# Attention scores whose second pass is made of 64-row products on alternating halves of the rows

## The chip, the cores and the metric

The kernel runs on one core of a Trainium2 chip. Its engines run side by side and wait for each other through semaphores: TensorE multiplies matrices (a weight load, then a product that streams the other operand through it), VectorE and ScalarE work on elements, GpSimd works on elements and starts some transfers, SyncE starts most transfers. The metric is device microseconds from start to end, the median of three runs.

## The reference

Three transformer layers on 512 tokens of width 1024: a retention layer, a layer of chunk attention and a hybrid layer, with squared-ReLU and gated MLPs between them. The change touches the attention of the second and third layer, in which each head's query and key have 64 features:

```python
# layer 2, 16 heads: own chunk of 64 tokens and the 8 before
s = jnp.einsum('bqhd,bkhd->bhqk', qb, kb).astype(jnp.float32) * scale + bias[None]
p = jax.nn.softmax(s, axis=-1).astype(vb.dtype)
return jnp.einsum('bhqk,bkhd->bqhd', p, vb)
# layer 3, 4 heads with relative bias, 4 with a forget gate, 8 with a window of 128
lg = jnp.einsum('bhqd,bhqkd->bhqk', qb, kg).astype(jnp.float32) * SCALE
```

All of it is in float32. The last line stands for the three branches of the hybrid layer, which differ in mask and bias.

## The kernel before

**Number format.** A float32 value is split into a high part that TensorE takes in its f32r type and a low part, the rest. A product is made of three: high by high, high by low, low by high. ScalarE makes the high part (a copy into an f32r tile), VectorE the low part (the value less its high part).

**The work.** Units of 128x1024 weights stream in through a ring of four buffers; `split` makes their high and low parts (ScalarE L1278, VectorE L1919) and `proj` multiplies them (24 products of 128x512, L617 to L619). In the attention stage (the trace shows it from 805 to 965 us) one step of a loop handles several heads at different places of the pipeline. The second block (1372 to 1520 us) has the 16 heads of the hybrid layer in the same manner.

**One head.** `proj` gives a tile of q or k for a pair of heads, 64 rows each; `qk_tile` (VectorE L2473) brings it to `af`. For half 0 or 1 of the pair `q_hi` (ScalarE L1596) writes q's high part to the half's own 64 rows of `q_st`, and `q_lo` (VectorE L2480) its low part to the other 64. `k_hi` (L1602) writes k's high part to both halves of `kh_st`, and `k_lo` (L2487) its low part to the own half of `kl_st`, whose other half `zero_rows` has set to zero once. So in `scores` one product of 128 rows against `kh_st` (L956) is high by high plus low by high, and a second against `kl_st` (L957) adds high by low, with zeros for 64 of its rows. This is done for four query tiles of 128 tokens, each with the keys it can see: 128, 256, 384 and 512 wide in full heads, 128, 256, 256 and 256 in the window heads, two products a tile, one after the other. Heads 4 to 7 of the second block add a mask with a third product (L960).

**After the scores.** `maxima` (VectorE L2441) adds the bias and takes row maxima, `exps` (ScalarE L1583) exponentiates, `inverse` (L2466) and `normalise` (GpSimd L2990) scale, `turn` (TensorE L977) transposes ten blocks into banks 5, 6 and 7, ScalarE (L1591) and VectorE (`turned_los`, L2455) split them, and `weigh` (TensorE L990, L992) multiplies with the values into bank 7. `o_part` (ScalarE L1607) and `o_sum` (VectorE L2499) read bank 7; the last two transposes of the next head, which write bank 7, wait for that `o_sum`.

**Order.** Every engine runs its own list, in the order in which the code writes it. TensorE in step s: `turn` of head s-1, `proj`, `weigh` of head s-1, `scores` of head s+1. VectorE in step s of the attention stage: `maxima` of head s; in odd steps (head_par 0) `q_lo` and `k_lo` of half 0; low parts, inverses, value parts (L2530); `split`; in odd steps `q_lo`, `k_lo` of half 1, then `o_sum` and `qk_tile`; in even steps `qk_tile`, then `o_sum`. In step 13 `o_sum` stands between that `q_lo` and `k_lo`. In the second block odd steps split half 1 ahead of `qk_tile` and `o_sum`, and even steps split half 0 last, after `qk_tile`, with `o_sum` between `q_lo` and `k_lo` in steps 2, 4 and 6; from pair 5 on only q is split, since the last eight heads share their keys. Two counters, `qk_hi` and `qk_lo`, order these parts: 3 and 2 counts a half.

Of the kernel before, what the change touches and what calls it, by code (L numbers as in the profile page):

```python
# [94 lines left out]

TURNED = [(5, 0), (6, 0), (7, 0), (6, 384)]
# [144 lines left out]
def build(nc, stream, x_t, cols, wf, f_bias, sinks, rel_pad, rel_2, c_rope, c_decay, c_sq, c_tri,  # L241
# [5 lines left out]
    with ExitStack() as ctx:  # L247
# [169 lines left out]
        zeroed = sem("zeroed")  # L417
# [106 lines left out]
        q_st, kh_st, kl_st = [r_at(0), r_at(1)], [r_at(2), r_at(3)], [r_at(4), r_at(5)]  # L524
        pt_h, pt_l = arena_r[:, 8 * S:8 * S + 1280], arena_r[:, 8 * S + 1280:8 * S + 2560]
# [84 lines left out]
        def _(pe):  # L610
# [332 lines left out]
            def scores(sm, hd, half, kind):  # L943
# [3 lines left out]
                if kind == "window":  # L947
                    places = [(2, 0), (2, 128), (3, 0), (3, 256)]
                else:
                    places = [(2, 0), (4, 0), (2, 128), (3, 0)]  # L950
                for t, (b, o) in enumerate(places):
                    w = (CP_W if kind == "window" else P_W)[t]
                    k0 = (t + 1) * P - w
                    dst = banks[b][:, o:o + w]
                    q = q_st[half][:, t * P:t * P + P]
                    pe.matmul(dst, q, kh_st[half][:, k0:k0 + w], start=True, stop=False, skip_group_check=True)  # L956
                    m = pe.matmul(dst, q, kl_st[half][:, k0:k0 + w], start=False, stop=kind != "key",  # L957
                                  skip_group_check=True)
                    if kind == "key":
                        m = pe.matmul(dst[:, w - P:w], sqr[:, 0, :], sqr[:, 2, :],  # L960
                                      start=False, stop=True, skip_group_check=True)
# [41 lines left out]
            def att_step(s, par, unit=True, late=True, early=True, half=None):  # L1003
# [18 lines left out]
                if early:  # L1022

                    wait(pe, att.qk_lo, s * 2 + 4)
                    wait(pe, att.biased, (s + 1) * 4)
                    if s.b == -1:
# [4 lines left out]
                        pe.wait_ge(zeroed, 2)  # L1031
# [54 lines left out]
            for s in range(-1, 17):  # L1086
# [24 lines left out]
                if s < 15:  # L1111
                    hd = s + 1
                    p = hd // 2
                    wait(pe, hyb.qk_lo, QK_LO[p] + QK_OF[p] * (hd % 2 + 1) // 2)
                    wait(pe, hyb.biased, 4 * hd)
                    if hd == 0:

                        pe.wait_ge(hyb_vl, 8)
                        pe.wait_ge(zeroed, 4)
# [136 lines left out]
        def _(act):  # L1256
# [641 lines left out]
        def _(dve):  # L1898
# [527 lines left out]
            def maxima(sm, hd, par, n_bias, kind, sink=None):  # L2426
# [3 lines left out]
                places = [(2, 0), (2, 128), (3, 0), (3, 256)] if window else [(2, 0), (4, 0), (2, 128), (3, 0)]  # L2430
# [45 lines left out]
            def q_lo(sm, half, hi_before):  # L2476

                a, b = HEAD * half, HEAD - HEAD * half
# [29 lines left out]
            def att_step(s, head_par, unit=False, late=True, early=True, pair=None, half=None, ended=None,  # L2508
# [5 lines left out]
                if sets and not head_par:  # L2514

                    q_lo(att, 0, s * 3 + 3)
                    k_lo(att, 0, s * 3 + 3)
# [31 lines left out]
                if sets and not head_par:  # L2549
                    q_lo(att, 1, s * 3 + 6)  # L2550
                    if part_between:
                        finish_head()
                    k_lo(att, 1, s * 3 + 6)
# [704 lines left out]
```

## Time and profile before

| What | Value |
|---|---|
| Median of three runs | 2068.41 us (2067.94 to 2068.67) |
| The profiled execution, its own time | 2069.39 us |
| Its span, first to last instruction | 2067.7 us |
| TensorE products busy | 2056.1 us, 10508 of them |
| VectorE busy | 1407.9 us |
| ScalarE busy | 993.9 us |
| GpSimd busy | 308.9 us |
| Granted TensorE clock | full (1.00) in every slice |

A product's busy time runs from its start to the end of its write-back, so neighbouring products overlap in the trace; how fast they follow each other is read from their starts. "PEld" in the rows is the weight load. A row's bracket gives the idle time of the engine ahead of the instruction and what ended it.

### The profile page before, as it was taken

The page shows a single profiled execution, that of the slowest core. Times are in us where ns is not written, and L with a number is a line of the kernel's source. Part 1 is how long each engine was busy: PE and PEld are TensorE (multiplying, and loading weights), DVE is VectorE, ACT ScalarE, POOL GpSimd, SP SyncE. Part 2 cuts the span into 40 slices and gives each one's busy share as a digit, 9 for nine tenths or more (in the row PEclk, how much of TensorE's full clock was granted, in tenths as well). Part 3 has the DMA queues.
Part 4 walks back from the last instruction along what each step waited for, and adds up shares of the span by engine and source line. Part 5 has one row for each costly group of instructions (what it writes and reads, how often), then busy time and mean ns, then how long its engine had stood idle before and what let it go on. Part 6 is the DMA issues. An engine that isn't in the chain of part 4 may idle for free.

```text
span 2067.7 us, 30244 instructions
## 1 busy us (share of the span) xinstructions
PE 2056.1 (99%) x10508; PEld 1759.1 (85%) x10508; DVE 1407.9 (68%) x2322; ACT 993.9 (48%) x1695; POOL 308.9 (15%) x329
## 2 busy tenths in 40 slices
PE   9999999999999999999999999999999999999998
PEld 7888888789989888888899898888888888888887
DVE  7464645687868653888778687577764477666674
ACT  5433434464554344786645442467652244433343
POOL 2122212210002121443100002413300020000000
PEclk9999999999999999999999999999999999999999
DMA  5232222224334233222142323232222223333322
GB/s 199 87 101 71 98 87 82 81 79 143 101 106 148 92 96 103 92 88 76 66 133 83 110 93 111 97 102 85 80 82 102 91 99 105 112 102 112 101 91 83
DMA packets 58502, 205.35 MB, mean 99 GB/s; under 512 B 7017, under 2 KB 8185, under 8 KB 58400
## 3 DMA queue, kind: packets, MB, share of 16 engines
q1 hardware_dynamic: 53504, 189.29, 27.4%
q0 software_dynamic: 4176, 13.52, 2.2%
q8 instruction: 64, 1.05, 0.2%
q10 hardware_dynamic: 720, 1.18, 0.2%
q14 instruction: 38, 0.31, 0.1%
HBM read 201.83 MB, written 6.07 MB: 101 GB/s over the span
## 4 chain that ended last, share of the span: by engine, by line
PE 94%; DVE 3%; ACT 1%; issue 1%; DMA 0%; POOL 0%; ACTq 0%; DVEq 0%
PE bank L617 30%; PE bank L618 30%; PE bank L619 30%; PE bank L977 1%; PE bank L992 1%; PE bank L956 1%; PE bank L990 1%; PE bank L957 1%; ACT arena L1583 1%; DVE w_lo L1919 0%; PE bank L672 0%; DMA h<-in_x_t 0%; DVE h L1979 0%; ACT w_hi L1278 0%; DVE arena L2441 0%
## 5 line engine op out<-in xcount | busy, mean ns | idle before, releaser
L617 PE MATMUL bank<-x_hi,w_hi 128*128 128x512 f32 x1544 | 604.3, 391 | 0.0
L618 PE MATMUL bank<-x_lo,w_hi 128*128 128x512 f32 x1552 | 604.2, 389 | 0.0
L619 PE MATMUL bank<-x_hi,w_lo 128*128 128x512 f32 x1544 | 601.1, 389 | 0.0
L1919 DVE TENSOR_TENSOR w_lo<-raw,w_hi 128x1024 fp32r<-128x1024 f32 x305 | 386.2, 1271 | 167.4 <-ACT w_hi L1278 167.3
L617 PE MATMUL bank<-arena_r,w_hi 128*128 128x256 f32 (+1 forms) x1296 | 430.7, 332 | 2.2 <-DVE h L1979 2.0
L619 PE MATMUL bank<-arena_r,w_lo 128*128 128x256 f32 (+1 forms) x1296 | 429.6, 331 | 0.0
L618 PE MATMUL bank<-arena_r,w_hi 128*128 128x256 f32 (+1 forms) x1280 | 423.4, 331 | 0.0
L1278 ACT ACTIVATE w_hi<-raw 128x1024 fp32r<-128x1024 f32 x305 | 318.5, 1051 | 160.5 <-PE bank L619 158.8
L618 PEld LDWEIGHTS bank<-x_lo,w_hi 128*128 128x128 f32 x1552 | 291.5, 188 | 59.4
L619 PEld LDWEIGHTS bank<-x_hi,w_lo 128*128 128x128 f32 x1544 | 289.9, 188 | 60.6
L617 PEld LDWEIGHTS bank<-x_hi,w_hi 128*128 128x128 f32 x1544 | 290.0, 188 | 59.1
L617 PEld LDWEIGHTS bank<-arena_r,w_hi 128*128 128x128 f32 x1296 | 246.2, 190 | 26.9 <-DVE h L1979 2.1
L619 PEld LDWEIGHTS bank<-arena_r,w_lo 128*128 128x128 f32 x1296 | 246.2, 190 | 23.2
L618 PEld LDWEIGHTS bank<-arena_r,w_hi 128*128 128x128 f32 x1280 | 243.2, 190 | 22.3
L1979 DVE TENSOR_TENSOR h<-bank,h 128x512 f32<-128x512 f32 x96 | 66.0, 689 | 116.7 <-PE bank L619 116.6
L2990 POOL TENSOR_SCALAR arena<-arena,small 128x256 f32<-128x256 f32 (+3 forms) x128 | 92.2, 733 | 217.1 <-DVE small L2466 172.6
L1973 DVE TENSOR_TENSOR arena<-bank,rbc 128x512 f32<-128x512 f32 x78 | 53.7, 689 | 100.7 <-PE bank L619 100.6
L1478 ACT ACTIVATE w_hi<-raw 128x512 fp32r<-128x512 f32 x96 | 58.7, 624 | 77.9 <-PE bank L619 65.9
L1830 ACT ACTIVATE arena<-arena,colv 128x512 f32<-128x512 f32 x44 | 35.9, 816 | 124.5 <-DVE arena L1973 124.5
L2300 DVE TENSOR_TENSOR arena<-bank,arena 128x256 f32<-128x256 f32 x186 | 76.0, 420 | 23.2 <-PE bank L619 21.8
L617 PE MATMUL bank<-w_hi,x_hi 128*128 128x512 f32 x208 | 80.9, 389 | 0.0
L618 PE MATMUL bank<-w_lo,x_hi 128*128 128x512 f32 x208 | 80.9, 389 | 0.0
(287 smaller groups left out, 2580.9 us busy)
## 6 DMA issues: line engine op xcount, KB each, us to landing
raw<-in_stream SPq DMA_DIRECT2D x354, 512.0 KB, 3.2
arena<-in_rel_pad POOLq DMA_DIRECT2D x16, 256.0 KB, 3.8
bias_strips<-bias_strip_once POOLq DMA_DIRECT2D x12, 320.0 KB, 4.2
h<-in_x_t SPq DMA_DIRECT2D x6, 256.0 KB, 8.3
arena<-in_c_decay POOLq DMA_DIRECT2D x4, 256.0 KB, 2.9
arena<-bias_strips POOLq DMA_DIRECT2D x4, 256.0 KB, 3.6
arena<-cum_rows POOLq DMA_DIRECT2D x4, 256.0 KB, 3.5
arena<-bias_strips POOLq DMA_DIRECT2D x8, 128.0 KB, 2.4
```

The lines of the kernel that those rows point to most:

```text
L617: pe.matmul(dst, lh, rh, start=start, stop=False, **kw)
L618: pe.matmul(dst, lh, rl, start=False, stop=False, **kw)
L619: return pe.matmul(dst, ll, rh, start=False, stop=stop, **kw)
L956: pe.matmul(dst, q, kh_st[half][:, k0:k0 + w], start=True, stop=False, skip_group_check=True)
L1278: act.activation(w_hi[:, u % RING, :], raw[:, u % RING, :], ACT.Copy).then_inc(hi_ready, 1)
L1478: act.activation(block_at(slot)[0], src, ACT.Copy).then_inc(done, 1)
L1830: act.activation(cy[2 * (pair.b % 2) + n], cz[2 * (pair.b % 2) + n][:, 2:S + 2], ACT.Identity, scale=col(k + (C_CW + 2 * 2 * PAIRS)), bias ...
L1919: dve.tensor_tensor(w_lo[:, s, :], raw[:, s, :], f32(w_hi[:, s, :]), ALU.subtract).then_inc(lo_ready, 1)
L1973: return dve.tensor_tensor(dst, bank[:, :], rbc[:, :], ALU.mult)
L1979: dve.tensor_tensor(h[:, j, :], src[:, :], h[:, j, :], ALU.add).then_inc(tile_read, 1)
L2300: dve.tensor_tensor(part, banks[bank][:, 0:QUARTER], part, ALU.add).then_inc(quarter_read, 1)
L2990: pool.tensor_scalar(pf[par][:, a:a + w], pf[par][:, a:a + w], rinv[par][:, t:t + 1], 1.0, ALU.mult, ALU.mult).then_inc(sm.probs, 1)
```

## The change

`scores` runs the four first-pass products in a row (L963), and then the four of the second pass (L970), which have 64 rows each. In the second pass even query tiles use one half of the rows and odd tiles the other (`q_rows`). For that q's high part has to lie in that half for the even tiles too, and k's low part in both halves. `q_hi` gets a second copy that puts the even tiles' high part into the other half; `q_lo` becomes two operations, which write the low part of the odd tiles to the other half and of the even tiles over the high part in the own half. `k_lo` writes k's low part to both halves (in the second one only the 384 columns that an even tile can need). `zero_rows` and its semaphore go; the counters have 4 and 4 counts a half. Only the first product into a bank carries the start flag.

```diff
-QK_OF = [4, 4, 4, 4, 4, 2, 2, 2]
-QK_LO = [0, 4, 8, 12, 16, 20, 22, 24]
-QK_HI_OF = [6, 6, 6, 6, 6, 2, 2, 2]
-QK_HI = [0, 6, 12, 18, 24, 30, 32, 34]
+QK_OF = [8, 8, 8, 8, 8, 4, 4, 4]
+QK_PARTS = [0, 8, 16, 24, 32, 40, 44, 48]
...
+        def q_rows(half, t):
+            return HEAD * half if t % 2 else HEAD - HEAD * half
+        def q_tiles(ap, a, t):
+            return ap[a:a + HEAD, :].rearrange("p (u t n) -> p u t n", t=2, n=P)[:, :, t, :]
...
-                    pe.matmul(dst, q, kh_st[half][:, k0:k0 + w], start=True, stop=False, skip_group_check=True)
-                    m = pe.matmul(dst, q, kl_st[half][:, k0:k0 + w], start=False, stop=kind != "key",
-                                  skip_group_check=True)
+                for t, dst, k0, k1, w in tiles:
+                    pe.matmul(dst, q_st[half][:, t * P:t * P + P], kh_st[half][:, k0:k1], start=places[t][1] == 0,
+                              stop=False, skip_group_check=True)
...
+                for t, dst, k0, k1, w in tiles:
+                    a = q_rows(half, t)
+                    m = pe.matmul(dst, q_st[half][a:a + HEAD, t * P:t * P + P], kl_st[half][a:a + HEAD, k0:k1],
+                                  start=False, stop=True, skip_group_check=True)
...
                 act.activation(q_st[half][a:a + HEAD, :], af[0][a:a + HEAD, :], ACT.Copy).then_inc(sm.qk_hi, 1)
+                act.activation(q_tiles(q_st[half], q_rows(half, 0), 0), q_tiles(af[0], a, 0), ACT.Copy)\
+                    .then_inc(sm.qk_hi, 1)
...
-                wait(dve, sm.qk_hi, hi_before + 1)
-                dve.tensor_tensor(q_st[half][b:b + HEAD, :], af[0][a:a + HEAD, :], f32(q_st[half][a:a + HEAD, :]),
-                                  ALU.subtract).then_inc(sm.qk_lo, 1)
+                for n, t in enumerate((1, 0)):
+                    wait(dve, sm.qk_hi, hi_before + (n + 1))
+                    dve.tensor_tensor(q_tiles(q_st[half], HEAD - q_rows(half, t), t), q_tiles(af[0], a, t),
+                                      f32(q_tiles(q_st[half], a, t)), ALU.subtract).then_inc(sm.qk_lo, 1)
...
-                wait(dve, sm.qk_hi, hi_before + 3)
-                dve.tensor_tensor(kl_st[half][a:a + HEAD, :], af[1][a:a + HEAD, :], f32(kh_st[half][a:a + HEAD, :]),
-                                  ALU.subtract).then_inc(sm.qk_lo, 1)
-
-            def zero_rows(n):
-
-                wait(dve, products_done, at.pe)
-                dve.memset(f32(kl_st[0])[HEAD:P, :], 0.0).then_inc(zeroed, 1)
-                dve.memset(f32(kl_st[1])[0:HEAD, :], 0.0).then_inc(zeroed, 1)
+                wait(dve, sm.qk_hi, hi_before + 4)
+                for b, w in ((a, S), (HEAD - a, S - P)):
+                    dve.tensor_tensor(kl_st[half][b:b + HEAD, 0:w], af[1][a:a + HEAD, 0:w],
+                                      f32(kh_st[half][a:a + HEAD, 0:w]), ALU.subtract).then_inc(sm.qk_lo, 1)
```

TensorE, the scores of a full attention head before the change, with the transposes behind them (`arena_r` holds q and k, the banks are the products' targets):

```order
L956 MATMUL bank2<-arena_r 128x128 [waits att_biased,att_qk_lo]
L957 MATMUL bank2<-arena_r 128x128
L956 MATMUL bank4<-arena_r 128x256
L957 MATMUL bank4<-arena_r 128x256
L956 MATMUL bank2<-arena_r 128x384
L957 MATMUL bank2<-arena_r 128x384
L956 MATMUL bank3<-arena_r 128x512
L957 MATMUL bank3<-arena_r 128x512
```

The same place after it:

```order
L963 MATMUL bank2<-arena_r 128x128 [waits att_biased,att_qk_lo]
L963 MATMUL bank4<-arena_r 128x256
L963 MATMUL bank2<-arena_r 128x384
L963 MATMUL bank3<-arena_r 128x512
L970 MATMUL bank2<-arena_r 128x128
L970 MATMUL bank4<-arena_r 128x256
L970 MATMUL bank2<-arena_r 128x384
L970 MATMUL bank3<-arena_r 128x512
```

The second products of the four tiles moved behind the first of all four; the shapes are those of the targets, and L970 reads 64 rows.

VectorE, an odd step of the attention stage before the change, from the value parts to the next `maxima`:

```order
L2530 TENSOR_TENSOR arena_r<-arena,arena_r 128x8x64 [waits stage_hi]
L2466 RECIPROCAL small<-small 128x2 [waits att_exp]
L1919 TENSOR_TENSOR w_lo<-raw,w_hi 128x1024 [waits hi_ready]
L2480 TENSOR_TENSOR arena_r<-arena,arena_r 64x512 [waits att_qk_hi]
L2487 TENSOR_TENSOR arena_r<-arena,arena_r 64x512 [waits att_qk_hi]
L2499 TENSOR_TENSOR arena<-bank,arena 64x512 [waits att_o_part]
L2473 SCALAR_TENSOR_TENSOR arena<-bank,rbc 128x512 [waits products_done,att_qk_lo]
```

And after it:

```order
L2536 TENSOR_TENSOR arena_r<-arena,arena_r 128x8x64 [waits stage_hi]
L2476 RECIPROCAL small<-small 128x2 [waits att_exp]
L1929 TENSOR_TENSOR w_lo<-raw,w_hi 128x1024 [waits hi_ready]
L2491 TENSOR_TENSOR arena_r<-arena,arena_r 64x2x128 [waits att_qk_hi] x2
L2499 TENSOR_TENSOR arena_r<-arena,arena_r 64x512 [waits att_qk_hi]
L2499 TENSOR_TENSOR arena_r<-arena,arena_r 64x384
L2505 TENSOR_TENSOR arena<-bank,arena 64x512 [waits att_o_part]
L2483 SCALAR_TENSOR_TENSOR arena<-bank,rbc 128x512 [waits products_done,att_qk_lo]
```

Four operations stand ahead of `o_sum` (L2499 before, L2505 after) where there were two; the same four stand in this step for half 0, behind `maxima`.

## Rows read from the trace of the kernel before

**Rows 1.** The page, part 1: busy time, share and count of TensorE.
```profile
PE 2056.1 (99%) x10508; PEld 1759.1 (85%) x10508; DVE 1407.9 (68%) x2322; ACT 993.9 (48%) x1695; POOL 308.9 (15%) x329
```

**Rows 2.** Busy time by stretch: window, its length, then busy us (count) by engine.
```profile
840.00:860.00 20.00, 20.00 (x109) 17.17 (x108) 17.39 (x44) 16.17 (x44) 8.87 (x13) 1.00 0.23 79
```

**Rows 3.** Timeline of TensorE's products, one full head: start us, us, instruction.
```profile
844.59 0.27 PE L956 MATMUL bank<-arena_r 128*128 128x128 f32 x1
844.70 0.28 PE L957 MATMUL bank<-arena_r 128*128 128x128 f32 x1
...
844.98 0.28 PE L957 MATMUL bank<-arena_r 128*128 128x256 f32 x1
845.10 0.34 PE L956 MATMUL bank<-arena_r 128*128 128x384 f32 x1
845.27 0.34 PE L957 MATMUL bank<-arena_r 128*128 128x384 f32 x1
...
845.69 0.39 PE L957 MATMUL bank<-arena_r 128*128 128x512 f32 x1
845.92 1.43 PE L977 MATMUL bank<-ident,arena 128*128 128x128 f32 x10
```

**Rows 4.** Timeline of the weight loads in the same head.
```profile
845.10 0.19 PEld L957 LDWEIGHTS bank<-arena_r 128*128 128x128 f32 x1
```

**Rows 5.** Timeline of products, a window head: its first and the next transpose.
```profile
1455.02 0.27 PE L956 MATMUL bank<-arena_r 128*128 128x128 f32 x1
...
1456.01 0.27 PE L977 MATMUL bank<-ident,arena 128*128 128x128 f32 x1
```

**Rows 6.** Timeline of VectorE, one odd step of the attention stage.
```profile
836.27 0.69 DVE L2499 TENSOR_TENSOR arena<-bank,arena 64x512 f32<-64x512 f32 x1 [0.74 <-ACT arena L1607]
...
842.23 0.69 DVE L2530 TENSOR_TENSOR arena_r<-arena,arena_r 128x512 fp32r<-128x512 f32 x1 [0.26 <-ACT arena_r L1625]
...
846.18 0.68 DVE L2499 TENSOR_TENSOR arena<-bank,arena 64x512 f32<-64x512 f32 x1
```

**Rows 7.** The transposes' line: idle time ahead of them, us and times, by releaser.
```profile
  DVE arena L2499: 3.3, 11
```

**Rows 8.** Timeline of TensorE around the products of 34 rows: products, then loads.
```profile
13.63 0.39 PE L672 MATMUL bank<-w_hi,x_lo 128*128 128x512 f32 x1
...
14.81 0.38 PE L728 MATMUL bank<-arena,rel_sb 34*12 34x128 f32 x2
...
13.95 0.10 PEld L727 LDWEIGHTS bank<-arena,rel_sb 34*12 34x12 f32 x2 [0.35 <-issue]
...
15.12 0.53 PEld L672 LDWEIGHTS bank<-w_hi,x_hi 128*128 128x128 f32 x3 [0.21 <-issue]
```

**Rows 9.** Groups of VectorE by shape, 820 to 940 us: count | busy, mean ns.
```profile
L2487 DVE TENSOR_TENSOR arena_r<-arena,arena_r 64x512 fp32r<-64x512 f32 x14 | 11.0, 784 | 0.4
L2480 DVE TENSOR_TENSOR arena_r<-arena,arena_r 64x512 fp32r<-64x512 f32 x14 | 10.4, 742 | 0.4
...
L2455 DVE TENSOR_TENSOR arena_r<-bank,arena_r 128x384 fp32r<-128x384 f32 x13 | 6.9, 534 | 0.0
...
L2455 DVE TENSOR_TENSOR arena_r<-bank,arena_r 128x256 fp32r<-128x256 f32 x13 | 5.3, 407 | 0.0
```

**Rows 10.** Timeline of the second block, steps 2 and 3: ScalarE, VectorE, GpSimd, TensorE.
```profile
1398.42 0.63 ACT L1596 ACTIVATE arena_r<-arena 64x512 fp32r<-64x512 f32 x1 [1.58 <-DVE arena L2473]
...
1400.87 0.68 DVE L2487 TENSOR_TENSOR arena_r<-arena,arena_r 64x512 fp32r<-64x512 f32 x1 [0.38 <-ACT arena_r L1602]
1401.59 0.69 DVE L2441 CUSTOM_DVE_ANT_0 arena<-bank,arena 128x512 f32<-128x512 f32 x1
...
1406.23 2.94 POOL L2990 TENSOR_SCALAR arena<-arena,small 128x512 f32<-128x512 f32 x4 [7.34 <-DVE small L2466]
...
1409.46 0.39 PE L977 MATMUL bank<-ident,arena 128*128 128x128 f32 x2
```

**Rows 11.** Timeline of VectorE in a window head's step: its `o_sum`.
```profile
1463.99 0.68 DVE L2499 TENSOR_TENSOR arena<-bank,arena 64x512 f32<-64x512 f32 x1 [0.76 <-ACT arena L1607]
```

More of the change, by code:

```diff
@@ L93 @@
 CT_AT, CT_W = [0, 256, 512, 768], [256, 256, 256, 128]
+SCORES = [(2, 0), (4, 0), (2, 128), (3, 0)]
+SCORES_WINDOW = [(2, 0), (3, 0), (2, 128), (3, 256)]
 TURNED = [(5, 0), (6, 0), (7, 0), (6, 384)]
@@ L416, in build @@
         stage_lo = sem("stage_lo")
-        zeroed = sem("zeroed")
         hyb_vh = sem("hyb_vh")
@@ L947, in scores @@
                 if kind == "window":
[L948 removed]
+                    places = SCORES_WINDOW
                 else:
[L950 removed]
+                    places = SCORES
+                tiles = []
                 for t, (b, o) in enumerate(places):
                     w = (CP_W if kind == "window" else P_W)[t]
[L953 to L961 removed]
+                    tiles.append((t, banks[b][:, o:o + w], (t + 1) * P - w, (t + 1) * P, w))
+                for t, dst, k0, k1, w in tiles:
+                    pe.matmul(dst, q_st[half][:, t * P:t * P + P], kh_st[half][:, k0:k1], start=places[t][1] == 0,
+                              stop=False, skip_group_check=True)
+                    if kind == "key":
+                        pe.matmul(dst[:, w - P:w], sqr[:, 0, :], sqr[:, 2, :],
+                                  start=False, stop=False, skip_group_check=True)
+                for t, dst, k0, k1, w in tiles:
+                    a = q_rows(half, t)
+                    m = pe.matmul(dst, q_st[half][a:a + HEAD, t * P:t * P + P], kl_st[half][a:a + HEAD, k0:k1],
+                                  start=False, stop=True, skip_group_check=True)
                 m.then_inc(sm.scores, 1)
@@ L1022, in att_step @@
                 if early:
-                    wait(pe, att.qk_lo, s * 2 + 4)
+                    wait(pe, att.qk_lo, s * 4 + 8)
                     wait(pe, att.biased, (s + 1) * 4)
@@ L1113, in _ @@
                     p = hd // 2
-                    wait(pe, hyb.qk_lo, QK_LO[p] + QK_OF[p] * (hd % 2 + 1) // 2)
+                    wait(pe, hyb.qk_lo, QK_PARTS[p] + QK_OF[p] * (hd % 2 + 1) // 2)
                     wait(pe, hyb.biased, 4 * hd)
@@ L2429, in maxima @@
                 window = kind == "window"
-                places = [(2, 0), (2, 128), (3, 0), (3, 256)] if window else [(2, 0), (4, 0), (2, 128), (3, 0)]
+                places = SCORES_WINDOW if window else SCORES
                 for part in WHOLE if window else sm.parts:
@@ L2514, in att_step @@
                 if sets and not head_par:
-                    q_lo(att, 0, s * 3 + 3)
-                    k_lo(att, 0, s * 3 + 3)
+                    q_lo(att, 0, s * 4 + 4)
+                    k_lo(att, 0, s * 4 + 4)
                 if late and head_par:
@@ L2549, in att_step @@
                 if sets and not head_par:
-                    q_lo(att, 1, s * 3 + 6)
+                    q_lo(att, 1, s * 4 + 8)
                     if part_between:
                         finish_head()
-                    k_lo(att, 1, s * 3 + 6)
+                    k_lo(att, 1, s * 4 + 8)
                 if late and not head_par and not part_between:
@@ L2569, in first_pair @@
                     qk_tile(sm, k, 0)
-                    if k == 0:
-                        zero_rows(n)
                 for half in range(2):
-                    q_lo(sm, half, 3 * half)
-                    k_lo(sm, half, 3 * half)
+                    q_lo(sm, half, 4 * half)
+                    k_lo(sm, half, 4 * half)
             sum_los(2)
@@ L2578, in _ @@
             columns_of(2)
-            first_pair(att, 0)
+            first_pair(att)
             for c in range(2):
@@ L2605, in _ @@
             columns_of(BOTH)
-            first_pair(hyb, 1)
+            first_pair(hyb)
             dve.wait_ge(wf_h, 1)
@@ L2661, in _ @@
                 if 0 <= s < 14 and s % 2:
-                    q_lo(hyb, 1, QK_HI[p] + QK_HI_OF[p] // 2)
+                    q_lo(hyb, 1, QK_PARTS[p] + QK_OF[p] // 2)
                     if p < 5:
-                        k_lo(hyb, 1, QK_HI[p] + QK_HI_OF[p] // 2)
+                        k_lo(hyb, 1, QK_PARTS[p] + QK_OF[p] // 2)
                 if s in HYB_UNITS:
                     at.step()
-                    qk_tile(hyb, HYB_UNITS[s], QK_LO[(s + 3) // 2])
+                    qk_tile(hyb, HYB_UNITS[s], QK_PARTS[(s + 3) // 2])
                 if 0 <= s < 14 and not s % 2:
-                    q_lo(hyb, 0, QK_HI[p])
+                    q_lo(hyb, 0, QK_PARTS[p])
                     if s in PART_BETWEEN:
@@ L2672, in _ @@
                     if p < 5:
-                        k_lo(hyb, 0, QK_HI[p])
+                        k_lo(hyb, 0, QK_PARTS[p])
                 if s in GATE_STEPS:
```

8 lines of the change are left out of this document (3 added, 5 removed).

## The prediction

> **What bounds the kernel now.** I read the page's busy shares first, then a stretch of the attention stage, then single instructions of one head, then what VectorE does between two heads. TensorE is busy 99% of the span [rows 1], so any change of its work shows unless something else hides it. In the attention stage VectorE is busy 17.39 of 20 us beside it [rows 2]: at 87% it has little room, and whether its new work is free depends on order, not on the sum.
>
> One head's scores take 1.33 us, from 844.59 to the first transpose at 845.92 [rows 3]. The products start 0.11 us apart where a 128-wide one is followed by a weight load (a load takes that long), 0.12 after a 256-wide, 0.17 after a 384-wide, 0.23 after a 512-wide. The load for the next product starts together with the running one: the load of L957 begins at 845.10, when L956 does [rows 3, 4]. A head of the window kind takes 0.99 us [rows 5].
>
> The second thing that binds is a lock between VectorE and TensorE. Call a step of the attention loop a splitting step if VectorE writes the low parts of both halves of a pair in it (att_step with s = 1, 3, ... 13). In the one from 836.27 VectorE works almost without a gap until it adds a head's output (o_sum, L2499) from 846.18 to 846.86 [rows 6]. TensorE's ten transposes began at 845.92 [rows 3]; at the 0.11 us of a 128-wide product eight of them take 0.88, and the last two need that o_sum because they write bank 7: TensorE is there at 846.8, just before VectorE is done. The trace counts 11 such waits of the transposes on L2499, 3.3 us [rows 7]. So the slack of VectorE in a splitting step is nil.
>
> **The change part by part.** *The products.* Pass 1 is the same four full-height products, now in a row: 0.11 + 0.12 + 0.17 and 0.21 of streaming for the 512-wide one, 0.61 us. Pass 2 has four 64-row products whose loads still follow each other: three spacings of 0.11 and 0.21 for the last, 0.54, since the wide ones can run on one half of the rows while the next loads on the other. The unknown is the change between full height and 64 rows, twice a head. The trace has one such place: the products of 34 rows, L727 and L728 [rows 8]. The full-height product before them starts at 13.63, and the next load, which elsewhere starts with it, starts at 13.95, 0.32 later. On the way back the last 34-row pass starts at 14.92 (half of the 14.81 pair, 0.11 wide), streams until 15.03, and the load of L672 starts at 15.12. In both directions the load waits some 0.1 us beyond the end of the streaming, and a full load of 0.11 is then uncovered: 0.2 us each way. These products are also plain f32 while the new ones are f32r, so the row is near, not the same. The other bound is no stall. I take 0.2, as the only row that changes the height.
>
> TensorE alone then: 0.61 + 0.2 + 0.54 + 0.2 = 1.56 against 1.33, +0.23 for each of 24 full heads; the window kind has 0.46 + 0.2 + 0.44 + 0.2 = 1.30 against 0.99, +0.31 for each of 8. Without a stall it is 0.61 + 0.54 = 1.15 (taken as 1.17 with the first load), -0.16, and 0.90, -0.09. If the two halves also load at once, pass 2 falls to its longer half, 256 + 512 columns, 0.34: 0.95, -0.38, and 0.68, -0.31.
>
> The Trainium skill, page "TensorEngine Tiling (Array Packing)", section "Key Properties", says that a change of tiling mode drains the engine. The 34-row products agree with it, though their type differs too; by that rule every head pays twice, and without it the sum below is 5.5 us lower.
>
> *VectorE.* For each half q_lo becomes two 64x256 operations instead of one 64x512, and k_lo gets a second of 64x384. A 64x512 takes 0.74 (L2480) and 0.78 (L2487); operations of the same kind take 0.407 at 256 and 0.534 at 384 wide [rows 9]; these are 128 rows high, but 512 wide ones cost 0.68 to 0.78 at either height, so I take them as they are. q: 2 x (0.41 + 0.035 between waits) against 0.78, +0.10. k: the second one follows without a wait and overlaps the first by 0.07, +0.47. Together +0.57 a half. From below, the two narrow ones could cost no more than the wide one and k +0.4; from above, k could cost a whole 0.78.
>
> *ScalarE.* One more copy of 64x256 for each half. A 64x512 copy takes 0.63 [rows 10]; I take 0.38, between half of it and the whole. ScalarE is busy 16.17 of 20 us [rows 2], so the sum is hidden, but VectorE waits for these copies in places.
>
> *The lock, attention.* In a splitting step the first +0.57 meets the gap of 0.26 before L2530 [rows 6], which waits for ScalarE, itself 0.38 later; what is left is about +0.4. The second +0.57 meets no gap. o_sum ends +0.97 later, TensorE waits that long, and what follows (proj, weigh, scores, the next o_sum) hangs on it: the shorter or longer scores before it are hidden, since TensorE waits anyway. Steps 1, 3, 5 and 7 give about 0.98 each, 3.9; steps 9 and 11, where that gap is under 0.1, 1.14 each, 2.3; in step 13 o_sum stands ahead of the second k_lo, 0.67. Sum 6.9 us. With the stall the scores of the step between end about 0.1 later than the o_sum beside them, 6 x 0.1 = 0.6.
>
> *Second block.* Here an even step ends with k_lo behind ScalarE's copies: L2487 starts at 1400.87 after a wait for L1602, and the next maxima (L2441) at 1401.59 [rows 10]. Both new pieces lie there, 0.38 + 0.47 = +0.85. Maxima, low parts, the weights' split, the inverse and GpSimd's scaling follow in a chain that ends at 1409.17 (1406.23 + 2.94), and the transposes start at 1409.46: slack 0.29, so +0.56 for that pair. By the same reading pair 0 has no slack (+0.85), pair 2 has 0.6 (+0.25, under TensorE's own two heads of +0.23, so 0.47) and pair 3 hardly any (+0.8). Sum 2.7. From head 8 on only q is split, +0.10 and a copy; VectorE waits 0.76 us for ScalarE ahead of an o_sum there [rows 11], which covers them.
>
> *Where TensorE alone decides.* Attention heads 0, 1, 14 and 15 and head 0 of the second block: 5 x 0.23 = 1.15; seven window heads (the eighth is in pair 3's wait): 7 x 0.31 = 2.2. The zeroing that falls away (two VectorE memsets for each block) lay long before the first scores, as do the first pair's added operations: nothing either way; uncovered it would be about 1 us each.
>
> Sum: 6.9 + 0.6 + 2.7 + 1.15 + 2.2 = +13.5 us. The profiled execution took 2069.4 (span 2067.7), 1.0 above the median of 2068.4: 2082.9 by the first, **2082** from the median.
>
> **The rivals.** *Lock, no stall.* If full height and 64 rows follow without a stall, TensorE gains, but only where it is not waiting: 6.9 + 2.5 - 5 x 0.16 - 7 x 0.09 = +8.0, 2076.4; with both halves loading at once +5.3, 2073.7. For it: the one row that shows a stall is of another type and has 34 rows and 12 columns, not 64 and 128.
>
> *Stall, no lock.* If the new VectorE work finds cover, only TensorE's part counts: 24 x 0.23 + 8 x 0.31 = +8.0, 2076.4. Against it: rows 6 and 7.
>
> *Faster.* The two halves load and multiply at once, no stall, and o_sum in the splitting steps is not later: -(24 x 0.38 + 8 x 0.31) = -11.6, 2056.8; with loads one after another -(24 x 0.16 + 8 x 0.09) = -4.6, 2063.8. It decides at a slack of about 1 us on VectorE in each splitting step, where the rows show none. The Trainium skill, same page and section, states that different tiles load weights and multiply in parallel; no row here shows it, and by it the forecast's pass 2 would be 0.2 shorter a head, which the lock hides in most of them.
>
> *The halves do not run together.* Then pass 2 is 0.61 instead of 0.54, and the forecast rises by 12 x 0.07, +0.8: within its range. *Nothing measurable*: half of the lock is covered and parallel halves give back the rest.
>
> **How the numbers follow.** Forecast 0.50, its own range 2078 to 2087 (VectorE's prices from below and above, a stall of 0.15 to 0.3); lock without stall 0.25 (2073 to 2078); stall without lock 0.08; faster 0.09; nothing 0.08. Low 2071 and high 2087 leave out the faster case, half of the nothing case and a little above, under 2 in 10. A change under 0.2%, 4.1 us, cannot be told from none here: faster (under 2064.3) 0.09, within 0.09, slower 0.82.
>
> **What would show it.** Right: TensorE's waits on o_sum grow from 3.3 to about 10 us, in the splitting steps by 1 us each; the load of the first 64-row product starts about 0.3 after the 512-wide one starts, and a like hole stands behind the last; the window heads take 1.3 us. VectorE's busy time rises by some 13 us. Wrong in the stall: loads start with the product before them, window heads at or under 0.9. Wrong in the lock: the transposes in splitting steps still take 1.2 to 1.4 us.

## The result and the profile after

The changed kernel takes 2082.89 us (median of 6 runs, 2082.66 to 2083.11), the kernel before 2068.57 on the same chip (6 runs, 2067.94 to 2068.77): a ratio of 1.0069 [1.0059, 1.0080], 14.3 us slower. The span of the profiled execution went from 2067.7 to 2081.0 us, +13.3.

Part 1 of the page of after, which answers to [rows 1]: busy time, share and count of each engine.

```profile
PE 2059.5 (99%) x10508; PEld 1749.1 (84%) x10508; DVE 1427.2 (69%) x2376; ACT 1004.6 (48%) x1727; POOL 308.3 (15%) x329
```

TensorE runs as many products as before. VectorE has 54 more operations and 19.3 us more work, half as much again as the forecast's 13.

**One full head on TensorE**, which answers to [rows 3, 4]. First the products, then the weight loads: start us, us, instruction, and in brackets the idle time ahead of it.

```profile
845.11 0.85 PE L963 MATMUL bank<-arena_r 128*128 128x128 f32 x4
845.89 0.62 PE L970 MATMUL bank<-arena_r 64*128 64x128 f32 x4
846.44 1.09 PE L987 MATMUL bank<-ident,arena 128*128 128x128 f32 x8
848.02 0.44 PE L987 MATMUL bank<-ident,arena 128*128 128x128 f32 x2 [0.48 <-DVE arena L2505]
```
```profile
845.05 0.53 PEld L963 LDWEIGHTS bank<-arena_r 128*128 128x128 f32 x4
845.89 0.30 PEld L970 LDWEIGHTS bank<-arena_r 64*128 64x128 f32 x4 [0.31 <-issue]
846.44 0.86 PEld L987 LDWEIGHTS bank<-ident,arena 128*128 128x128 f32 x8 [0.25 <-issue]
```

The loads have a hole on each side of L970, for which the profile shows no releaser ("issue"). Single records give its size: the last L963 product starts at 845.564 and the first L970 load at 845.889, 0.325 later; the last L970 product starts at 846.117 and the next load at 846.441, 0.324 later. That is the 0.32 of the 34-row products [rows 8]. It is not one fixed time, though: in the window heads, where 256-wide products stand ahead of both changes, the two starts are 0.206 and 0.204 apart, and in heads 4 to 7 of the second block, where the 128-wide mask product ends the first pass, 0.151. From these three, an estimate: the hole is about 0.06 us for each 128 columns of the product ahead of it and 0.1 on top, which is the forecast's reading of [rows 8], that the load waits some 0.1 us beyond the streaming.

Inside L970 something else is to be seen: the four loads start at 845.889, 845.892, 845.997 and 846.001, the products at 845.891, 845.894, 846.054 and 846.117. Two loads start 3 ns apart, and two products run at once. So from the first product to the first transpose the scores take 846.44 - 845.11 = 1.33 us, what they took before [rows 3]: what the two halves give by running together, the two changes of height take. The last row of the first block is the other part of the loss: the two transposes that write bank 7 wait 0.48 us for `o_sum` (L2505).

A window head, products, which answers to [rows 5]:

```profile
1475.82 0.68 PE L963 MATMUL bank<-arena_r 128*128 128x128 f32 x4
1476.42 0.50 PE L970 MATMUL bank<-arena_r 64*128 64x128 f32 x4
1476.86 0.98 PE L987 MATMUL bank<-ident,arena 128*128 128x128 f32 x7
```

It takes 1476.86 - 1475.82 = 1.04 us against 0.99: +0.05, where the forecast had +0.31.

**Waits of TensorE**, the view of waits in after: line <- releaser: us in total, times, longest.

```profile
PEld bank L970 <- issue: 7.0, 24, 0.3
PEld bank L1000 <- DVE arena_r L2536: 6.2, 7, 1.4
PEld bank L987 <- DVE arena L2505: 6.0, 10, 0.9
PEld bank L987 <- issue: 5.6, 19, 1.1
PEld bank L987 <- POOL arena L2994: 4.5, 5, 1.3
```

The first row is the change to 64 rows and the fourth, but for its longest wait of 1.1, the change back; idle time under 0.15 us is left out of the view, and with it the window heads. The same view of before has 1.3 us (5) for `weigh` on the value parts (L1000 and L2536 now, L990 and L2530 then), 2.5 us (8) for the transposes on `o_sum` and 0.8 us (3) on GpSimd's scaling. So the second row is new in size, and no step of the forecast names it.

[rows 7], 3.3 us in 11, is another view: it adds up the idle time of products and of loads, so that some waits stand in it twice. In after it has, for the transposes and `o_sum`:

```profile
  DVE arena L2505: 9.7, 18
```

That is the forecast's "about 10 us", by the same count.

**VectorE**, groups by shape from 820 to 950 us, which answer to [rows 9]: count | busy, mean ns.

```profile
L2491 DVE TENSOR_TENSOR arena_r<-arena,arena_r 64x256 fp32r<-64x256 f32 x27 | 13.6, 502 | 0.8
L2499 DVE TENSOR_TENSOR arena_r<-arena,arena_r 64x512 fp32r<-64x512 f32 x14 | 10.0, 718 | 0.0
...
L2499 DVE TENSOR_TENSOR arena_r<-arena,arena_r 64x384 fp32r<-64x384 f32 x14 | 7.9, 564 | 0.4
L2536 DVE TENSOR_TENSOR arena_r<-arena,arena_r 128x512 fp32r<-128x512 f32 x7 | 6.8, 966 | 0.1
```

The order of VectorE in one odd step, from `maxima` to the next `maxima`, which answers to [rows 6]:

```profile
837.03 0.69 DVE L2451 CUSTOM_DVE_ANT_0 arena<-bank,arena 128x512 f32<-128x512 f32 x1
...
842.72 1.01 DVE L2536 TENSOR_TENSOR arena_r<-arena,arena_r 128x512 fp32r<-128x512 f32 x1
...
844.96 1.10 DVE L2491 TENSOR_TENSOR arena_r<-arena,arena_r 64x256 fp32r<-64x256 f32 x2
845.98 1.27 DVE L2499 TENSOR_TENSOR arena_r<-arena,arena_r 64x512 fp32r<-64x512 f32 x2
847.28 0.68 DVE L2505 TENSOR_TENSOR arena<-bank,arena 64x512 f32<-64x512 f32 x1
...
848.49 0.67 DVE L2451 CUSTOM_DVE_ANT_0 arena<-bank,arena 128x512 f32<-128x512 f32 x1
```

In this step a half's q takes 1.04 to 1.10 us where one operation took 0.74, and its k 1.27 where it took 0.78 [rows 9]: about +0.8 a half. The value parts, which the change does not touch, went from 0.77 (mean of 7 in before) to 0.97.

**The second block**, which answers to [rows 10]; the second row of GpSimd is the head shown there, the first the head before it: GpSimd, VectorE, TensorE.

```profile
1405.97 2.07 POOL L2994 TENSOR_SCALAR arena<-arena,small 128x512 f32<-128x512 f32 x4 [4.49 <-DVE small L2476]
...
1416.80 3.33 POOL L2994 TENSOR_SCALAR arena<-arena,small 128x512 f32<-128x512 f32 x4 [8.21 <-DVE small L2476]
```
```profile
1408.76 0.87 DVE L2491 TENSOR_TENSOR arena_r<-arena,arena_r 64x256 fp32r<-64x256 f32 x2 [0.70 <-ACT arena_r L1604]
...
1410.86 1.27 DVE L2499 TENSOR_TENSOR arena_r<-arena,arena_r 64x512 fp32r<-64x512 f32 x2 [0.48 <-ACT arena_r L1612]
1412.16 0.69 DVE L2451 CUSTOM_DVE_ANT_0 arena<-bank,arena 128x512 f32<-128x512 f32 x1
...
1416.79 1.26 DVE L2491 TENSOR_TENSOR arena_r<-arena,arena_r 64x256 fp32r<-64x256 f32 x2
1417.97 1.46 DVE L2499 TENSOR_TENSOR arena_r<-arena,arena_r 64x512 fp32r<-64x512 f32 x2
```
```profile
1420.19 1.31 PE L987 MATMUL bank<-ident,arena 128*128 128x128 f32 x10 [0.92 <-POOL arena L2994]
```

GpSimd's same four operations take 2.07 us when VectorE is not splitting q and k, and 3.33 when it is; before they took 2.94 in this place [rows 10]. VectorE's same two take 0.87 us with GpSimd idle and 1.26 beside the scaling. The transposes wait for that scaling.

**Where the time is lost.** For each kernel I took the start of the same TensorE product in its trace and in that of before, less the two spans' starts. The difference is the delay, in us, at four points:

| Kernel | first attention scores | attention's last transposes | after the second block's k pairs | end |
|---|---|---|---|---|
| after | -0.9 | 8.2 | 12.7 | 13.4 |
| TensorE's part alone | 0.2 | 0.2 | 0.5 | 1.2 |
| the preparation alone | -0.2 | 9.0 | 13.7 | 13.5 |
| q's preparation alone | -0.1 | 2.8 | 3.3 | 3.3 |
| k's preparation alone | -0.6 | 6.6 | 9.8 | 9.8 |
| order of the products alone | -0.6 | -0.6 | -0.5 | -0.6 |
| 64 rows, all on one half | -0.6 | 1.9 | 4.4 | 6.5 |
| after, `o_sum` earlier | -0.3 | 13.5 | 18.0 | 18.7 |
| before, `o_sum` earlier | -0.4 | 0.3 | 0.3 | 0.4 |
| after, k's second part on GpSimd | -0.5 | 3.5 | 8.0 | 8.6 |

The first column is what the starts of two executions differ by. From the first column to the last after loses 14.2 us: 9.1 in the attention stage, 4.5 in the pairs of the second block and 0.65 in the window heads.

### The profile page after: what moved, and what is told of

Its sections match the earlier page's. It is cut to its first block, busy times and chain, and to the rows that moved or that the text cites. A ratio compares the mean times of both kernels' runs of the same rounds, so it can differ in the third digit from the quotient of the medians.

```text
span 2081.0 us, 30318 instructions
## 1 busy us (share of the span) xinstructions
PE 2059.5 (99%) x10508; PEld 1749.1 (84%) x10508; DVE 1427.2 (69%) x2376; ACT 1004.6 (48%) x1727; POOL 308.3 (15%) x329
## 3 DMA queue, kind: packets, MB, share of 16 engines
q8 instruction: 64, 1.05, 0.2%
## 4 chain that ended last, share of the span: by engine, by line
PE 90%; DVE 5%; ACT 2%; issue 2%; POOL 1%; DMA 0%; DVEq 0%; ACTq 0%; POOLq 0%
PE bank L624 29%; PE bank L625 29%; PE bank L626 29%; POOL arena L2994 1%; PE bank L987 1%; ACT arena L1591 1%; DVE w_lo L1929 1%; DVE arena_r L2499 1%; DVE arena L2451 1%; PE bank L679 1%; DVE arena_r L2491 0%; PE bank L1002 0%; DVE arena_r L2465 0%; PE bank L1000 0%; ACT w_hi L1286 0%
```

## Experiments

The theory of the forecast is that VectorE's added operations are what TensorE waits for; its main rival is that the 64-row products themselves cost the time. Each expectation below is as it stood before its kernel ran.

**TensorE's part alone.** q and k are prepared as before, the second pass is that of after. With the rows laid out as before, the even tiles' second products meet zeros and miss high by low.

```diff
-                    pe.matmul(dst, q, kh_st[half][:, k0:k0 + w], start=True, stop=False, skip_group_check=True)
-                    m = pe.matmul(dst, q, kl_st[half][:, k0:k0 + w], ...)
+                    pe.matmul(dst, q_st[half][:, t * P:t * P + P], kh_st[half][:, k0:k1], start=places[t][1] == 0, ...)
...
+                    a = q_rows(half, t)
+                    m = pe.matmul(dst, q_st[half][a:a + HEAD, t * P:t * P + P], kl_st[half][a:a + HEAD, k0:k1], ...)
```

> TensorE's part alone: the kernel before with the new order of scores and 64-row second products, but q's and k's parts prepared as before, so in even query tiles the second product meets zeros and q's high part by k's low part is left out there. Theory A (the added VectorE and ScalarE work costs the time, the new products cost next to nothing because both halves load and stream at once and give back the two stalls of a head): a full head's scores 1.33 us as before and 0.06 more in the transposes behind them, a window head +0.11, together +1 to +2.5 us, 2069.5 to 2071. Rival B (the prediction's price: +0.23 a full head, +0.31 a window head): +4 to +8, 2072.5 to 2076.5.

Measured: 2069.82 us, ratio 1.0006 [0.9997, 1.0016]. The view of waits of this kernel (L972 is the second pass, L989 the transposes):

```profile
PEld bank L972 <- issue: 6.9, 24, 0.3
...
PEld bank L989 <- DVE arena L2511: 2.0, 7, 0.5
```

The hole of the height change is there in full, and yet the kernel is no more than 1.3 us slower; the delay grows almost only in the window heads, 0.1 each. The products give back what the holes take, and the transposes' wait on `o_sum` stays at its old size.

**The preparation alone.** q and k are prepared as in after, the second pass runs at full height as before, with the 128 columns of k's other half that nobody fills set to zero. The second pass then adds low by low.

```diff
-                    m = pe.matmul(dst, q_st[half][a:a + HEAD, t * P:t * P + P], kl_st[half][a:a + HEAD, k0:k1],
+                    m = pe.matmul(dst, q_st[half][:, t * P:t * P + P], kl_st[half][:, k0:k1],
```

> The preparation alone: the changed kernel with its second products at full height (128 rows), which adds low by low and leaves nothing out; the 128 columns of k's rest that no operation writes are zeroed once. Theory A: nearly the whole loss, +10.5 to +13, 2079 to 2081.5, with TensorE's waits on the output sum and on the value parts as in the changed kernel. Rival B: the lock as priced, +9.4 less what the shorter products change, at most 2078.

Measured: 2082.25 us, ratio 1.0066 [1.0049, 1.0083], +13.7 of after's +14.3, a little above the range of theory A. Its delay follows that of after through the attention and the k pairs, and stands still in the window heads. The two experiments settle the main question: the loss is the preparation, not the products.

**q's and k's preparation apart.** In the first kernel ScalarE's second copy of q and the two `q_lo` are those of after, k as before; in the second k's low part is written to both halves, q as before. The products are those of before. In the first the even tiles get low by low in place of high by low, in the second all tiles get low by low besides.

```diff
+                act.activation(q_tiles(q_st[half], q_rows(half, 0), 0), q_tiles(af[0], a, 0), ACT.Copy).then_inc(sm.qk_hi, 1)
...
+                for n, t in enumerate((1, 0)):
+                    dve.tensor_tensor(q_tiles(q_st[half], HEAD - q_rows(half, t), t), ...)
```

> q's part of the preparation alone: the second copy on ScalarE and the low part in two operations; k and the products as before, so even tiles get low by low instead of high by low. Theory A (every microsecond of VectorE ahead of the output sum is paid, and ScalarE's copy delays VectorE in the second block): the pair takes about 1.07 instead of 0.78 us a half, +0.29, which is 0.58 in each of 7 odd steps plus 0.42 of ScalarE in four pairs of the second block: +4 to +7, 2072.5 to 2075.5. Rival C (as predicted, q costs 0.10 a half): +1 to +3, 2069.5 to 2071.5.

```diff
+                for b, w in ((a, S), (HEAD - a, S - P)):
+                    dve.tensor_tensor(kl_st[half][b:b + HEAD, 0:w], af[1][a:a + HEAD, 0:w],
+                                      f32(kh_st[half][a:a + HEAD, 0:w]), ALU.subtract).then_inc(sm.qk_lo, 1)
```

> k's part of the preparation alone: the second operation of k's low part into the other half; q and the products as before (low by low is added, nothing left out). Theory A: +0.49 a half, 0.98 in each of 6 odd steps less what gaps cover, and 0.5 in the pairs of the second block: +5 to +8, 2073.5 to 2076.5. If the two parts simply add, e3 and e4 together make e2; if a gap covers the first microsecond of either, e2 is more than their sum.

Measured: q 2072.25 us, 1.0018 [1.0008, 1.0028], +3.7; k 2079.08 us, 1.0051 [1.0034, 1.0068], +10.6. Together 14.3, which is what both cost at once (13.7): in sum they add up. By stage they do not: in the attention stage q loses 2.9 and k 7.2, both together 9.2, and in the pairs of the second block 0.5 and 3.2, both together 4.7. So that the sum fits is in part chance. q lies below the range of theory A and above that of rival C; k alone costs more than was expected of it. k's waits (lines as in before):

```profile
PEld bank L977 <- DVE arena L2500: 5.7, 10, 0.8
PEld bank L990 <- DVE arena_r L2531: 5.4, 7, 1.0
PEld bank L977 <- POOL arena L2991: 3.5, 5, 1.1
```

Fourteen added operations in the attention stage hold TensorE in two places of a step, at `o_sum` and at `weigh`, and in the second block behind GpSimd's scaling. In this trace a half's k takes 1.38 us on average (single records, first start to last end) against 0.78 before: 14 x 0.60 = 8.4 us, against 7.2 of delay in that stage (-0.6 to 6.6). Most of what VectorE takes longer, TensorE loses. k's part is VectorE's alone; q's also has ScalarE's second copy, and no run divides the two. With q alone VectorE's wait for ScalarE ahead of the value parts grows from 1.3 to 2.2 us.

**The order of the products alone.** Full height as before, but the four first products ahead of the four second ones.

```diff
-                    m = pe.matmul(dst, q, kl_st[half][:, k0:k0 + w], start=False, ...)
+                for t, dst, k0, k1, w in tiles:
+                    m = pe.matmul(dst, q_st[half][:, t * P:t * P + P], kl_st[half][:, k0:k1], start=False, ...)
```

> The order of the products alone: the kernel before with the four first products in a row and then the four second ones, all at full height. If the order itself costs or gains nothing (theory A): a head's scores 1.33 us, no hole in the weight loads, 2068 to 2069.5. If the loads behind the 512-wide product or the order of the banks mattered: beyond 1 us either way.

Measured: 2068.79 us, 1.0001 [0.9991, 1.0010]. The order by itself is worth nothing, and without a change of height there is no hole: in the head from 844.04 the last first product starts at 844.490 and the next load at 844.492.

**64 rows, all on one half.** The preparation of before, which holds q's high part and k's low part in the half's own rows; the second pass has 64 rows, but every tile uses the same ones. The edit is shown against the kernel with TensorE's part alone.

```diff
-                    a = q_rows(half, t)
+                    a = HEAD * half
```

> 64-row second products, all on the half's own rows, with the preparation of the kernel before (that half holds q's high part and k's low part already, so nothing is left out). Theory A (two stalls of 0.2 us a head, which only the halves' running at once gives back): pass 2 takes 0.61 instead of 0.35 us, a full head 1.6 us, a window head 1.3, in all +8 to +10, 2076.5 to 2078.5. Rival D (a stall that is no price of the height, or halves that gain nothing by running at once): the same as e1, 2069 to 2071.

Measured: 2075.88 us, 1.0035 [1.0022, 1.0049], +7.3, under the +8 to +10 that theory A expected and far from rival D. Products of one full head in it:

```profile
844.78 0.85 PE L965 MATMUL bank<-arena_r 128*128 128x128 f32 x4
845.56 0.90 PE L972 MATMUL bank<-arena_r 64*128 64x128 f32 x4
846.40 1.31 PE L989 MATMUL bank<-ident,arena 128*128 128x128 f32 x10
```

The second pass takes 846.40 - 845.56 = 0.84 us where after has 0.55. The hole ahead of it is the same. This is the bare price of the height change: a full head takes 1.62 against 1.33 before, and the window heads add 0.33 each by the delay. Those 0.29 are near the forecast's +0.23 and the 0.33 near its +0.31, which were reckoned for loads that follow each other; what after gains on this kernel is that its halves load together. In the attention stage only 2.5 us show, since the wait on `o_sum` hides part.

**`o_sum` earlier.** If the place of `o_sum` behind the four added operations is the fault, moving it should help. In odd steps `o_sum` goes between half 1's `q_lo` and `k_lo` (as step 13 has it), and half 0's `k_lo` goes behind the value parts and the inverses; ScalarE's `o_part` moves with `o_sum`; once on after, once on before.

```diff
-                part_between = half is not None and sets
+                part_between = late and sets and not head_par
...
                     q_lo(att, 0, s * 4 + 4)
-                    k_lo(att, 0, s * 4 + 4)
...
+                if sets and not head_par:
+                    k_lo(att, 0, s * 4 + 4)
```

> The changed kernel with two pieces moved in the odd steps of the attention stage: half 0's k_lo behind the value parts and the inverses, and half 1's k_lo behind the output sum (as step 13 has it already). Theory A: the waits of TensorE on the value parts and on the output sum shrink by the 1.2 us that each k_lo takes, the attention stage loses 2 to 5 us instead of 9, in all 2075 to 2079. Rival E (VectorE's sum in an odd step binds, wherever the pieces stand): at least 2081.

> The same two pieces moved in the kernel before. Theory A: the odd steps' waits of 0.1 to 0.4 us on the output sum and the 1.3 us on the value parts go, -1 to -4 us, 2064.5 to 2067.5. Rival E: no change, or a loss where the next step's maxima start later.

Measured: on after 2087.86 us, 1.0093 [1.0077, 1.0108], 5.0 worse than after; on before 2069.72, 1.0005 [0.9995, 1.0014], nothing. The first was expected to win most of the attention's loss back and did the opposite. Its waits, and VectorE in one odd step:

```profile
PEld bank L987 <- POOL arena L2995: 10.5, 11, 1.3
...
PEld bank L987 <- DVE arena L2505: 6.8, 10, 1.9
PEld bank L1000 <- DVE arena_r L2535: 4.5, 7, 0.8
```
```profile
838.22 0.69 DVE L2451 CUSTOM_DVE_ANT_0 arena<-bank,arena 128x512 f32<-128x512 f32 x1
...
842.37 0.17 DVE L2476 RECIPROCAL small<-small 128x2 f32<-128x2 f32 x1 [0.92 <-ACT arena L1591]
...
843.78 0.69 DVE L2535 TENSOR_TENSOR arena_r<-arena,arena_r 128x512 fp32r<-128x512 f32 x1 [0.26 <-ACT arena_r L1635]
...
848.13 0.68 DVE L2505 TENSOR_TENSOR arena<-bank,arena 64x512 f32<-64x512 f32 x1
848.85 1.54 DVE L2499 TENSOR_TENSOR arena_r<-arena,arena_r 64x512 fp32r<-64x512 f32 x2
850.43 0.69 DVE L2483 SCALAR_TENSOR_TENSOR arena<-bank,rbc 128x512 f32<-128x512 f32 x1
851.03 0.68 DVE L2451 CUSTOM_DVE_ANT_0 arena<-bank,arena 128x512 f32<-128x512 f32 x1
```

What stands behind `o_sum` now is k's low part, `qk_tile` and the next head's maxima; the exponentials and GpSimd's scaling hang on these maxima, and the next transposes on the scaling. The wait on GpSimd went up by 6.0 us (4.5 to 10.5), and that on `o_sum` did not even fall. The rows show why: in after half 0's `k_lo` filled the time in which VectorE would have waited for ScalarE, and here it stands idle instead, 0.92 us until the exponentials (L1591) let it take the inverses and 0.26 ahead of the value parts. Over the stage its wait for the exponentials grows from 5.0 us (9) to 9.2 (13). So the odd step lasts 12.8 us from one `maxima` to the next (838.22 to 851.03) where after has 11.5 (837.03 to 848.49), and `o_sum` starts 9.9 us behind `maxima` in place of 10.25, not the 1.3 us earlier that half 1's `k_lo` takes. On before the same exchange shows small: 1.2 us (3) left on `o_sum`, 4.4 us (11) on GpSimd, and 8.3 us (14) of VectorE's wait for the exponentials where there were 5.4 (10). Two pieces were moved at once and idle time came with them, so whether the place of `o_sum` alone binds stays open. What the run shows is that TensorE pays when VectorE's row of an odd step gets longer, by idle time as by work.

**k's second part on GpSimd.** If the length of VectorE's row is what TensorE pays for, work that leaves it must come back. In the attention stage k's 64x384 operation goes to GpSimd, half 0 ahead of the scaling of an odd head, half 1 behind it.

```diff
-                for b, w in ((a, S), (HEAD - a, S - P)):
+                for b, w in ((a, S), (HEAD - a, S - P))[0:2 if rest else 1]:
...
+            def k_rest(half, hi_before):
+                pool.wait_ge(att.qk_hi, hi_before + 4)
...
+                pool.tensor_tensor(kl_st[half][b:b + HEAD, 0:S - P], af[1][a:a + HEAD, 0:S - P],
+                                   f32(kh_st[half][a:a + HEAD, 0:S - P]), ALU.subtract).then_inc(att.k_rest, 1)
```

> The changed kernel, but in the attention stage the second low part of k (64x384, the copy for the other half of the rows) is made by GpSimd instead of VectorE: half 0 ahead of the scaling of an odd head, half 1 behind it; the second block is unchanged. If VectorE's added time in the odd steps is what costs (theory A), 14 operations of about 0.5 us leave its row, o_sum and the value parts come 0.5 to 1 us earlier in each of seven steps, and most of the 7 us that k's part cost in this stage comes back: 2075 to 2078. If the copy itself is what has to be waited for, or GpSimd's scaling is pushed back by it and VectorE's operations slow down beside it (theory B), there is no gain or a loss: 2081 or more, with TensorE's transposes waiting for the scaling instead of o_sum.

Measured: 2077.92 us (2076.56 to 2078.66), 1.0043 [1.0029, 1.0057]: 5.0 better than after. First GpSimd's group of it, 820 to 950 us, then the waits (L988 are the transposes, L1001 `weigh`):

```profile
L3014 POOL TENSOR_TENSOR arena_r<-arena,arena_r 64x384 fp32r<-64x384 f32 x14 | 17.5, 1253 | 3.7 <-ACT arena_r L1614 2.1 <-issue 0.4 <-POOL arena L2999 0.3
```
```profile
PEld bank L988 <- POOL arena L2999: 5.6, 8, 1.3
...
PEld bank L1001 <- DVE arena_r L2541: 3.6, 7, 0.8
PEld bank L988 <- DVE arena L2510: 3.3, 9, 0.8
```

GpSimd needs 1.25 us for what VectorE does in 0.56, and still the attention's delay falls from 9.1 to 4.0 us: the waits on `o_sum` go from 6.0 to 3.3 us and those on the value parts from 6.2 to 3.6, while GpSimd's scaling takes 1.1 more. So in the attention stage most of the loss was VectorE's time. Since TensorE's products bring nothing, this version too stays behind the kernel before.

## Why the forecast came out, and where its steps were off

The time, the sign and the place were as forecast, but the sum fits to a microsecond because errors of opposite sign offset each other, which is luck.

**The change of height: right.** Its load was forecast some 0.3 after the start of the last wide product, on both sides, from one row of products with 34 rows in another type [rows 8]; 0.325 and 0.324 were measured. The Trainium skill, page "TensorEngine Tiling (Array Packing)", section "Key Properties", says that a change of tiling mode drains the engine; the holes of this trace agree, 0.15 to 0.33 us at a change of height against 0.002 with the order of the products alone.

**The second pass: too dear.** The step that failed is "Pass 2 has four 64-row products whose loads still follow each other". The loads come in pairs 3 ns apart, and the second pass with the hole behind it takes 0.55 where the forecast had 0.54 + 0.2. A full head cost nothing instead of +0.23, a window head +0.05 in itself and 0.1 with the load behind it instead of +0.31. Of the terms 1.15 and 2.2, the kernel with TensorE's part alone showed 1.3 together. The Trainium skill, page "TensorEngine Tiling (Array Packing)", section "Key Properties", states that different tiles load and multiply in parallel; the forecast gave it beside its sum, since no row of before showed it. The trace of after has that row, 3 ns from load to load, and it agrees.

**VectorE's price: too low.** +0.57 a half was forecast, about +0.8 came. k's +0.47 was near (0.48 in most halves, 0.53 on average). q's +0.10 was not: two operations of 64x256 take 0.50 each on average, not 0.41. The row that I took [rows 9, L2455] reads one of its inputs from a bank, and the new operations read both from SBUF. In after's trace they take 0.87 for two when GpSimd is idle and 1.26 when it scales. The single records of the whole trace say the same: the 23 operations of 64x256 with no element operation of GpSimd beside them take 0.417 to 0.423 us, the 41 others 0.53 on average and up to 0.81, while the 48 operations of 128x256 that read a bank (L2465) take 0.41 to 0.43, beside GpSimd or not. So 0.41 was right for the operation by itself, and what it left out is the neighbour, which stretches too (2.07 and 3.33 us for GpSimd's four). The Trainium skill, page "GPSIMD Engine Reference", section "Specifications", gives a reason: GpSimd's access to SBUF, the on-chip memory that holds the arena, is shared with VectorE, with contention for operations that have two SBUF inputs. The trace agrees with it, by the two groups above; no run here takes the GpSimd work away to show it alone.

**The lock in the attention stage: right in place, incomplete.** 6.9 + 0.6 + 4 x 0.23 = 8.4 us was forecast, 9.1 came. It is made up differently. The heads at the ends cost nothing; the odd steps lost more, since the larger price met the same lack of slack. And half of the loss sits where the forecast named no wait of TensorE: `weigh` on the value parts, 6.2 us over 7 waits, beside 6.0 on `o_sum`. The forecast saw VectorE's gap of 0.26 ahead of those parts [rows 6] as cover, and overlooked that what exceeds it is waited for right there, and that they become longer themselves (0.77 to 0.97).

**The second block: right chain, mis-sized.** 2.7 us was forecast for the four pairs and 0.23 for head 0; 4.5 came. In the pair of [rows 10] the maxima came later by about 0.85, as forecast (1401.59 to 1412.16, less the delay of 9.7 that the kernel already had there, is 0.87). What the term lacked is GpSimd's scaling: 3.33 us in place of 2.94, since VectorE's next four operations run beside it. Less the slack of 0.29 this makes 0.87 + 0.39 - 0.29 = 0.97; 1.05 was measured for that pair.

**The window heads: cover right.** `q_lo` and its copy are hidden there: with the preparation alone the delay does not grow at all (13.7 to 13.5). TensorE's own term was the mis-sized one, 2.2 against 0.65.

So the terms were off by +1.6 on the second block, +0.7 on the attention and -1.6 on the window heads. The rival without a stall in which both halves load at once was half true: they do, the stall is there as well, and the two cancel.

What stays open: whether the hole can be shared by two heads (second passes of both heads of a pair in one stretch) was not tried; nor why the load waits some 0.1 us beyond the streaming; nor what part of q's loss is ScalarE's copy; nor what `o_sum` ahead of half 1's `k_lo` would give if half 0's stayed where it is.

## What to carry to other kernels

Work that makes the busiest engine's products cheaper has to be prepared by another engine; look at that engine's row for a whole step, not at the wait it shows today, because without slack most of every added microsecond comes out somewhere. Before moving an operation, see whose wait it covers where it stands: here the move left VectorE idle for 1.2 us of an odd step. Price an added operation from a row with the same kinds of inputs and the same neighbour running, since the same two VectorE operations took 0.87 or 1.26 us here. Before cutting products to half height, count the changes of height: two a head took back all that the halves running together gave.

## What was not expected of the hardware

Two 64-row products on different halves load 3 ns apart and run at once, while the change between full height and 64 rows costs a hole from the last product's start to the next load in either direction, 0.32 us after a 512-wide product and 0.21 after a 256-wide one; with all products on one half (no loading together) the second pass takes 0.84 instead of 0.55 us. And GpSimd's four scalings stretched from 2.07 to 3.33 us when VectorE split q and k beside them, while VectorE's operations with an input from a bank kept their time.
